# Applying the norm factor of the up half at the residual instead of at every inner tile

## The reference, cut to what matters

```python
def rms_norm(x, g):
    y = xf * lax.rsqrt(jnp.mean(xf * xf, axis=-1, keepdims=True) + EPS)
    return y * g

def swiglu(h, w_in, w_out):            # w_in: 1024 x 5632, w_out: 2816 x 1024
    gu = h @ w_in
    gate, up = gu[..., :D_FF], gu[..., D_FF:]
    return (jax.nn.silu(gate) * up) @ w_out

for l in range(DEPTH):
    x = x + 0.5 * swiglu(rms_norm(x, g[0]), ffn_w_in[l, 0], ffn_w_out[l, 0])
    x = x + (s5_mixer(rms_norm(x, g[1])) if l < N_A else mla_attention(rms_norm(x, g[1]), ...))
    x = x + 0.5 * swiglu(rms_norm(x, g[2]), ffn_w_in[l, 1], ffn_w_out[l, 1])
    if l == N_A - 1: k, v = shared_kv(x, ...)
return rms_norm(x, final_norm)
```

## Time and profile before

| | |
|---|---|
| median of 3 timed runs | 1961.33 us (1961.1 to 1962.72) |
| span of the profiled execution, first to last instruction | 1960.5 us |
| PE busy | 1873.7 us, 96% of the span |
| DVE busy | 998.9 us, 51% |
| ACT busy | 590.6 us, 30% |
| POOL busy | 266.5 us, 14% |
| mean granted clock of PE | 0.973 of full |

### The profile page before, as it was taken

The page is one execution under the profiler, slowest core; times in us unless marked ns, Lnnn a source line. Parts: engine busy times, 40 slices in busy tenths (PEclk is TensorE's granted clock), DMA queues, the critical chain, the costliest instruction groups (busy, mean ns, idle before and its releaser), DMA issues.

```text
span 1960.5 us, 22646 instructions
## 1 busy us (share of the span) xinstructions
PE 1873.7 (96%) x8196; PEld 1494.7 (76%) x8196; DVE 998.9 (51%) x1306; ACT 590.6 (30%) x794; POOL 266.5 (14%) x171
## 2 busy tenths in 40 slices
PE   8887999998999999999999999999899999999996
PEld 5665887785888888888878888888655778888885
DVE  7889358725645544442285444323744354444224
ACT  5122222222233332331153323212424342323213
POOL 7456105301301300000020000000200100000001
PEclk8999999999999999999999999999969999999998
DMA  4244425565632222222222222222100122222221
GB/s 161 92 142 139 137 97 164 152 250 176 195 123 96 97 96 96 96 97 96 97 86 96 96 96 96 97 97 96 65 22 1 65 97 96 96 96 96 97 96 54
DMA packets 79398, 207.93 MB, mean 106 GB/s; under 512 B 24576, under 2 KB 32896, under 8 KB 77296
## 3 DMA queue, kind: packets, MB, share of 16 engines
q1 hardware_dynamic: 75440, 187.86, 28.5%
q0 software_dynamic: 2752, 17.24, 2.6%
q10 hardware_dynamic: 1152, 2.10, 0.3%
HBM read 184.10 MB, written 23.07 MB: 106 GB/s over the span
## 4 chain that ended last, share of the span: by engine, by line
PE 80%; DVE 12%; issue 4%; ACT 2%; POOL 1%; DMA 0%; DVEq 0%; SPq 0%; ACTq 0%; POOLq 0%
PE bank L1356 24%; PE bank L1358 24%; PE bank L1357 23%; DVE w_split L912 2%; PE bank L1670 1%; PE bank L1669 1%; DVE h_split L932 1%; PE bank L1691 1%; ACT w_split L604 1%; DVE gate L925 1%; PE bank L1552 1%; PE bank L1559 1%; PE bank L1673 1%; PE bank L1388 1%; PE bank L1682 1%
## 5 line engine op out<-in xcount | busy, mean ns | idle before, releaser
L912 DVE TENSOR_TENSOR w_split<-w_raw,w_split 128x1024 fp32r<-128x1024 f32 x302 | 390.5, 1297 | 684.2 <-ACT w_split L604 679.0
L1356 PE MATMUL bank<-h_split,w_split 128*128 128x512 f32 x1488 | 586.4, 394 | 21.2 <-DVE gate L923 13.3
L1357 PE MATMUL bank<-h_split,w_split 128*128 128x512 f32 x1488 | 581.5, 391 | 0.0
L1358 PE MATMUL bank<-h_split,w_split 128*128 128x512 f32 x1488 | 581.3, 391 | 0.0
L604 ACT ACTIVATE w_split<-w_raw 128x1024 fp32r<-128x1024 f32 x302 | 316.5, 1055 | 723.7 <-PE bank L1358 719.7
L1356 PEld LDWEIGHTS bank<-h_split,w_split 128*128 128x128 f32 x1488 | 281.1, 189 | 87.8 <-DVE gate L923 11.9
L1356 PE MATMUL bank<-g_split,w_split 128*128 128x512 f32 (+1 forms) x856 | 335.8, 392 | 7.0 <-DVE gate L923 3.6
L1357 PE MATMUL bank<-g_split,w_split 128*128 128x512 f32 (+1 forms) x856 | 334.7, 391 | 0.0
L1358 PE MATMUL bank<-g_split,w_split 128*128 128x512 f32 (+1 forms) x856 | 334.5, 391 | 0.0
L1358 PEld LDWEIGHTS bank<-h_split,w_split 128*128 128x128 f32 x1488 | 280.8, 189 | 59.1
L1357 PEld LDWEIGHTS bank<-h_split,w_split 128*128 128x128 f32 x1488 | 281.0, 189 | 58.8 <-issue 1.0
(11 more groups left out here) (243 smaller groups left out, 1254.2 us busy)
## 6 DMA issues: line engine op xcount, KB each, us to landing
w_raw<-wstream SPq DMA_DIRECT2D x302, 512.0 KB, 3.2
op_slots<-s_ops POOLq DMA_DIRECT2D x5, 2048.0 KB, 8.3
s_ops<-ops_out SPq DMA_DIRECT2D x8, 1024.0 KB, 4.4
op_slots<-s_ops SPq DMA_DIRECT2D x3, 2048.0 KB, 8.3
s_ops<-c_pow POOLq DMA_DIRECT2D x8, 512.0 KB, 4.2
s_ops<-k_window SPq DMA_DIRECT2D x64, 64.0 KB, 3.3
x_res<-xT SPq DMA_DIRECT2D x8, 256.0 KB, 8.2
bc_in<-bcd POOLq DMA_DIRECT2D x8, 256.0 KB, 5.5
```

Source lines behind the costliest of these rows:

```text
L912: tt(W[:, r, 1, :], RAW[:, r, :], W[:, r, 0, :].bitcast(F32), ALU.subtract).then_inc(s_lo, 1)
L1356: mm(bank, hi, x_hi, start=start, stop=True, skip_group_check=True)
L1357: mm(bank, hi, x_lo, start=False, stop=True, skip_group_check=True)
L1358: return mm(bank, lo, x_hi, start=False, stop=True, skip_group_check=True)
```

## The change

The factor is no longer multiplied into the up half of every inner tile. `gated` scales the gate half only, and the product with silu takes the up half straight from its PSUM bank. Both banks are now free only when that product is done, so the signal that PE waits for moves there. `add_ffn` takes over the factor: it makes 0.5 times the output bank times RSTD in UT, waits for that, adds UT to X, and waits again before UT is written anew.

```diff
@@ semaphores
-    s_read, s_silu, s_prod = sem("gate_up_read"), sem("silu_done"), sem("gated")
+    s_gate, s_silu, s_read = sem("gate_scaled"), sem("silu_done"), sem("gate_and_up_read")
@@ ScalarE, gate(stage, f)
+                act.wait_ge(s_gate, F + 1)
+                nc.scalar.activation(GT[:], GT[:], ACT.Silu).then_inc(s_silu, 1)
                 act.wait_ge(s_read, F + 1)
-                nc.scalar.activation(GT[:], GT[:], ACT.Silu).then_inc(s_silu, 1)
-                act.wait_ge(s_prod, F + 1)
                 nc.scalar.activation(gt_part(f, 0), GT[:], ACT.Copy).then_inc(s_g_hi, 1)
@@ VectorE, gated(stage, f, par, packs_done)
-                tt(UT[:], ub[:], RSTD[:], ALU.mult)
-                tt(GT[:], gb[:], RSTD[:], ALU.mult).then_inc(s_read, 1)
+                tt(GT[:], gb[:], RSTD[:], ALU.mult).then_inc(s_gate, 1)
                 dve.wait_ge(s_silu, F + 1)
-                tt(GT[:], GT[:], UT[:], ALU.mult).then_inc(s_prod, 1)
+                tt(GT[:], GT[:], ub[:], ALU.mult).then_inc(s_read, 1)
                 dve.wait_ge(s_g_hi, F + 1)
@@ VectorE, add_ffn(stage, d)
                 wait_acc(dve, stage, d)
-                stt(X[:, d, :], out_bank(stage, d)[:], 0.5, X[:, d, :], ALU.mult, ALU.add).then_inc(s_x, 1)
+                link(stt(UT[:], out_bank(stage, d)[:], 0.5, RSTD[:], ALU.mult, ALU.mult))
+                tt(X[:, d, :], X[:, d, :], UT[:], ALU.add).then_inc(s_x, 1)
+                dve.wait_ge(s_x, X_BASE[stage] + d + 1)
```

## The result

| | before | after |
|---|---|---|
| median of the timed runs | 1961.63 us (1961.1 to 1962.72, 4 runs) | 1978.4 us (1975.72 to 1979.54, 4 runs) |
| span of the profiled execution | 1960.5 us | 1976.2 us |
| mean granted clock of PE | 0.973 | 0.967 |

The ratio after/before is 1.0087, 95% interval 1.0075 to 1.0099, so 14.7 to 19.4 us more. The change makes the kernel slower. The forecast was 1979.8. The profiled execution grew by 15.7 us, and its own timed run took 1977.75.

The account below looks back on a forecast made before the run. PE bounds the kernel, busy 96% of the span; DVE work matters only where PE waits for it. Terms 3.0 + 3.0 + 6.3 + 6.3 + 2.4 - 2.5 = +18.5; 1960.5 + 18.5 + 0.8 = 1979.8 us; 8-in-10 range 1971 to 1985.

Parts of the forecast that it names:

- The pairs: Scale-then-add pairs at block ends: 0 behind FFN0A1, +3.0 us each behind FFN0A2 and FFN1B, +6.3 each behind FFN0B and FFN1A.
- The late read: Last tile's banks at FFN0A2, FFN0B, FFN1A, FFN1B: read 0.50 us late, 0.6 each, +2.4 us in all.
- The gain of the first stages: FFN0A1 and FFN0A2: DVE time saved in inner tiles moves PE only by -2.5 us (3.3 less 0.78).
- The first five tiles: FFN0A1 up to about 110 us: DVE runs ahead while POOL pauses, 5 x 0.60 = 3.0 us gained.
- so the loop DVE, POOL, PE keeps its period: First two stages: POOL's next block waits for DVE's coefficients behind held instructions, so the period gains nothing.
- Only while POOL pauses can DVE run ahead: First two stages: gain limited to FFN0A1's first five tiles, 3.0 us, and some 0.3 from a shrinking hold.
- For FFN0A2 I take 0: FFN0A2: no gain, because its long wait at 366 us sits behind an instruction held by POOL.
- The saved time turns into a longer hold: Inner tiles beside POOL: L927, ready 0.6 to 0.7 us earlier, still ends where it ended, held by POOL.
- the full 9.8 us: First two stages: the port rule read alone promises 9.8 us from the product L925 reading PSUM; the sum would be 1970.0.
- (a): First stages: DVE's time counts about half, as it slips ahead of POOL; about 11 us gained, 1971; chance 0.11.
- (b): First stages: all 21.5 us of DVE carried, PE's waits shrink, three clock falls avoided give 6; 1954.8; chance 0.04.
- (c): Slower passages, KVD's first column and sums of squares: PE's clock falls to 1.2 GHz, adding 1.0 + 7.8; 1988.6; chance 0.05.

## Why the prediction was right

It was right in direction and in size (1979.8 forecast, 1978.4 measured). By its own steps:

- *The pairs, +18.6.* Measured 19.7 from the landmarks, and 19.0 (16.1 to 22.0) by the kernel with the additions only. The pitch of 1.44 and the steps of 2.1 came out as rows 7 gave them. FFN0B and FFN1A: 6.4 each against 6.3. FFN0A2 and FFN1B: 3.5 and 3.4 against 3.0. There the last two passes of PE took 1.12, behind a wait, instead of the 0.86 that I had used. The pairs behind FFN0A1 were hidden, as said.
- *The late read, +2.4.* Right in place and size: a wait of 0.38 and a first matmul of 0.50, where 0.50 of each were forecast. From landmark to landmark it shows as 0.7 at FFN1A and 0.6 at FFN1B. At FFN0B 1.5 lie between the landmarks, of which asking for the two banks separately took back 1.1.
- *The gain of the first stages, -2.5.* This term was mis-sized. With FFN0A2's share of the late read the prediction had -1.9 at the first addition of FFN0A2, and -7.0 was measured. The first five tiles were right: 3.0 forecast, 2.6 gained at POOL's second block. The steps that failed are "so the loop DVE, POOL, PE keeps its period", the "Only" in "Only while POOL pauses can DVE run ahead", and "For FFN0A2 I take 0": the period fell by 0.9 us, four times over, which is 3.6. "The saved time turns into a longer hold" was true for the instruction removed, which shortened those periods by 0 to 0.1 each, but not for the product that changed its kind. I had reasoned from the low part L927 alone and had seen only how POOL holds DVE, not how DVE's product holds POOL, whose busy time fell with the product's freedom from 149 to 143 us. Up to 2.4 more came from the shorter stretches at half clock behind two waits, and these are not shown to belong to the change.

The Trainium skill ("SBUF — State Buffer", section "Who interferes with whom") says of the port pair that the two engines share: "Issue order, not op shape, decides who blocks." The traces agree that it goes both ways, by the 5.8 us that POOL got back (149.0 to 143.2). Of the two readings of that rule in the prediction, the full 9.8 us and nothing certain, the measured 4.2 lies between.

- *The rivals.* (a) Half of DVE's time, 11 us: 8.4 were gained before the late reads, but 6.0 without the clock's share, so its "half" was a quarter. Neither it nor my own term had the size. (b) had its waits wrong: those of 8.95, 3.58 and 3.73 us were still 8.46, 3.81 and 3.33. Of its clock part something showed, up to 2.4 us, though not because the waits had gone. (c) was half right: the clock fell in both columns, but its price was hidden, and in the sums of squares it did not fall.
- *The sum.* 18.5 forecast and 15.7 in the profiled execution: 5.1 too little gain, 1.1 too little for the pairs, about 1.0 too little between the landmarks. 5.1 - 1.1 - 1.0 = 3.0, the difference of 2.8 up to rounding. Another 0.75 was hidden around the span: the prediction took 0.8 us there, from a profile and timed runs of different executions, and the executions with both have about 1.6 (1977.75 less 1976.2 is 1.55). That the total came within 1.4 us is therefore in part luck; the costs were understood, the gain was not.

What stays open: whether the longer stretches at half clock in the one trace of the kernel before are typical of it, how the 4.2 us of the freed product split between DVE's shorter product and POOL's shorter instructions, and what makes the attention part vary by 6 us from one trace to the next.

## What to carry to other kernels

Price an edit by the place where its engine is waited for, not by its count: 88 instructions saved were worth 2 us, and 40 two-step additions at five block ends cost 19. Where two engines hold each other, the kind of operand matters more than the number of instructions, and the hold must be read from both sides. Before a multiplication is moved to a serial place, look whether it fits into a wait that its own engine already has: here the gap of 0.70 us for silu took it for nothing, and that version was 7 us faster than the kernel before and 24 faster than the change.

## What the runs showed of the hardware that was not expected

- A DVE instruction of 128x512 with one PSUM operand that writes back into its PSUM bank took 0.69 us, as long as one that writes SBUF (0.68). The next one, which did not wait for it, started 0.60 behind it; 0.72 was seen where one wrote SBUF and the next waited for it.
- PE's clock fell to 0.50 in a passage of three matmuls per 2.11 us (1.90 us busy in the 4 us before 990), and stayed at 1.00 in one of two passes per 1.45 us (9.24 us busy in 11). At half clock three matmuls take 1.65 of the 2.11 us (2.11 less the wait of 0.46), so in this passage, which DVE paces, the fall cost nothing.
- How long PE stayed at half clock behind the same wait differed between executions: a mean of 0.50 over 6 us before and 0.72 in the kernel with the same inner tiles and only the additions changed.
- With the product in SBUF or in PSUM, POOL's own instructions from 40 to 400 us took 148.8 to 151.0 us or 142.5 to 144.4: the hold between DVE and POOL has to be read on both.
- The attention part, which no experiment touched, took 538.1 to 544.4 us, with PE's clock at 0.83 in the window from 1450 to 1500 us before and 0.71 after. One look cannot tell 3 us of change from this.
